# Gate scratch of a hybrid decoder step: from one block of memory per key group to one per pair of token blocks

## The reference

```python
s = einsum('thik,hink->thin', q, sub_keys)
s_top, i_top = top_k(s, 16)
cand = s_top[:, :, 0, :, None] + s_top[:, :, 1, None, :]
best_s, best_c = top_k(cand, 16)
eid = i1 * 128 + i2
g = softmax(best_s)
act = gelu(einsum('thkd,td->thk', u_tab[eid], tb))
out = einsum('thk,thkd->td', (g * act), v_tab[eid])
```

## Time and profile before

| | |
|---|---|
| Median of 3 runs | 2411.62 us (2409.38 to 2411.7) |
| The profiled execution's own time | 2407.87 us |
| Its span in the profile | 2406.0 us |
| PE busy | 2380.0 us (99%) |
| DVE, ACT, POOL busy | 1607.6, 837.2, 1432.2 us |
| Moved by DMA | 510.01 MB, mean 212 GB/s |
| `gate_scratch`: stores, loads | 56 of 512 KB; 30 of 896 KB and 2 of 832 KB |

### The profile page before, as it was taken

How to read it: one execution, slowest core, us unless ns; L and a number is a source line. 1 busy time by engine, 2 the same in 40 slices (tenths; PEclk the granted TensorE clock), 3 DMA queues, 4 the chain that set the end, 5 groups by cost and what they waited for, 6 DMA issues and landing times.

```text
span 2406.0 us, 38105 instructions
## 1 busy us (share of the span) xinstructions
PE 2380.0 (99%) x14550; PEld 2214.3 (92%) x14550; DVE 1607.6 (67%) x2611; ACT 837.2 (35%) x1279; POOL 1432.2 (60%) x787
## 2 busy tenths in 40 slices
PE   9999999999999999999999999999999999999998
PEld 8999999987899999999999999999989999999997
DVE  7865444455874353279897688888576766666664
ACT  4433223332231011233343355655433333333332
POOL 5554434332444555457676667777667777777762
PEclk9999999999999999999999999999999999999999
DMA  5224222237742233247776769999988888888872
GB/s 212 82 76 137 97 97 97 96 120 239 263 152 90 80 123 95 93 152 273 243 248 235 255 194 314 300 302 304 333 315 315 311 314 326 313 311 322 318 258 75
DMA packets 207742, 510.01 MB, mean 212 GB/s; under 512 B 15856, under 2 KB 104304, under 8 KB 205168
## 3 DMA queue, kind: packets, MB, share of 16 engines
q1 hardware_dynamic: 115552, 236.75, 30.9%
q10 hardware_dynamic: 55184, 137.07, 15.3%
q0 software_dynamic: 36864, 134.23, 15.0%
HBM read 424.55 MB, written 83.44 MB: 211 GB/s over the span
## 4 chain that ended last, share of the span: by engine, by line
PE 91%; DVE 5%; DMA 2%; ACT 1%; issue 1%; DVEq 0%; SPq 0%; ACTq 0%
PE ps L886 52%; PE ps L633 29%; PE ps L934 4%; DMA cxb<-parked_tiles 1%; DVE prev L1687 1%; PE ps L899 1%; PE ps L805 1%; PE ps L792 1%; PE ps L800 1%; PE ps L809 1%; PE ps L825 1%; PE ps L658 0%; DMA gbuf<-gate_scratch 0%; PE ps L778 0%; DVE hu_lo L1516 0%
## 5 line engine op out<-in xcount | busy, mean ns | idle before, releaser
L582 POOL TENSOR_SCALAR w_hi<-raw 128x1024 fp32r<-128x1024 f32 x129 | 138.9, 1076 | 520.8 <-issue 390.2
L609 POOL TENSOR_TENSOR w_lo<-raw,w_hi 128x1024 fp32r<-128x1024 f32 x128 | 324.3, 2534 | 188.3 <-PE ps L886 187.5
L609 POOL TENSOR_TENSOR w_lo<-raw,e_hi 128x1024 fp32r<-128x1024 f32 x128 | 324.5, 2535 | 177.8 <-PE ps L886 170.2
L886 PE MATMUL ps<-p_hi,w_lo 128*128 128x448 f32 x1024 | 376.2, 367 | 0.0
L886 PE MATMUL ps<-g_hi,w_lo 128*128 128x448 f32 x1024 | 375.6, 367 | 0.0
L584 POOL TENSOR_TENSOR w_lo<-raw,w_hi 128x1024 fp32r<-128x1024 f32 x129 | 318.5, 2469 | 10.8
L633 PE MATMUL ps<-h_hi,w_hi 128*128 128x296 f32 (+1 forms) x1216 | 274.3, 307 | 1.6 <-ACT ma L1201 1.6
L633 PE MATMUL ps<-h_lo,w_hi 128*128 128x296 f32 (+1 forms) x1216 | 262.5, 297 | 0.0
L633 PE MATMUL ps<-h_hi,w_lo 128*128 128x296 f32 (+1 forms) x1216 | 262.1, 297 | 0.0
L1295 ACT ACTIVATE e_hi<-raw 128x1024 fp32r<-128x1024 f32 x128 | 135.9, 1061 | 261.5 <-DMA raw<-units 120.4
L633 PEld LDWEIGHTS ps<-h_hi,w_hi 128*128 128x128 f32 x1216 | 196.1, 188 | 26.5 <-issue 23.8
(11 more groups left out here) (332 smaller groups left out, 5430.8 us busy)
## 6 DMA issues: line engine op xcount, KB each, us to landing
raw<-units SPq DMA_DIRECT2D x385, 512.0 KB
gate_scratch<-gt SPq DMA_DIRECT2D x56, 512.0 KB
activation_scratch<-ge ACTq DMA_DIRECT2D x120, 224.0 KB
abuf<-activation_scratch ACTq DMA_DIRECT2D x30, 896.0 KB, 5.8
gbuf<-gate_scratch ACTq DMA_DIRECT2D x30, 896.0 KB
prev<-ssm_in ACTq DMA_DIRECT2D x8, 1024.0 KB, 6.7
ssm_s<-prev ACTq DMA_DIRECT2D x8, 1024.0 KB, 4.5
parked_tiles<-stage ACTq DMA_DIRECT2D x24, 296.0 KB, 2.1
```

The lines of the kernel that those rows point to most:

```text
L582: pool.tensor_scalar(w_hi[:, s, :], raw[:, r, :], 1.0, 1.0, ALU.mult, ALU.mult).then_inc(s_whi, 1)
L609: pool.tensor_tensor(w_lo[:, n % 2, :], raw[:, n % RAW, :], e_hi[m % HS_].bitcast(F32), ALU.subtract)\
L886: last = mm(accp[par], w[:, k * P:(k + 1) * P], x_[:, k, t0:t0 + ND], start=k == 0 and i == 0, stop=k == KT - 1 and i == 2)
```

## The change

The DRAM tensor `gate_scratch` gets another order of dimensions: pair of token blocks, partition, key group, where it was key group, partition, pair of token blocks. The bytes, the tiles on the chip and the order and number of all instructions stay. A store now writes 8 key groups that lie behind one another: one run of 4096 bytes per partition, where it was 8 runs of 512 bytes. A load now reads one run of 512 bytes per partition and pair of blocks: 14 (13 for group 0) per partition, 2 MB apart, where it was one run of 7168 bytes (6656 for group 0).

```diff
-    gate_dram = nc.dram_tensor("gate_scratch", [2 * NG, P, NB // 2, GI // 2 * SB], F32).ap()
+    gate_dram = nc.dram_tensor("gate_scratch", [NB // 2, P, 2 * NG, GI // 2 * SB], F32).ap()
...
-                sp_.dma_start(gate_dram[gs, :, B].rearrange("g p a -> p g a"),
+                sp_.dma_start(gate_dram[B, :, gs],
                               gt[:, B % 2].rearrange("p (g i) t -> p g (i t)", g=2 * NG)[:, gs]).then_inc(s_gs[B % 2], 16)
...
                 act.dma_start(gbuf[:, hb, 0:blocks].rearrange("p b i t -> p b (i t)"),
-                              gate_dram[bass.ds(g * 2 + hb, 1), :, 0:blocks].rearrange("a p b i -> (a p) b i"))\
+                              gate_dram[0:blocks, :, bass.ds(g * 2 + hb, 1)].rearrange("b p a i -> p b (a i)"))\
                     .then_inc(s_gl[hb], 16)
```

## The result

| | before | changed |
|---|---|---|
| Median of 6 runs each | 2411.66 us | 2429.24 us |
| Lowest and highest | 2405.44 to 2416.41 | 2422.1 to 2433.66 |
| The profiled execution's own time, span | 2407.87, 2406.0 | 2433.66, 2431.6 |

The ratio is 1.0070, with a 95% interval from 1.0052 to 1.0087: slower by some 17 us, where 6.5 us were forecast. In a later measurement, of 6 more runs, the changed kernel had 2426.02 us, 1.0067 [1.0043, 1.0092]. Its profiled execution there took 2417.59 us with a span of 2415.7. That is 16 us from the one shown here, and the reason is part of what follows.

What follows compares the result with a forecast made beforehand. PE was taken to bound the kernel, busy for 2380.0 of 2406.0 us. Terms 0 + 5 + 1.5 + 0 = 6.5 us gave 2414.4 for the profiled execution and 2418 us against the median; range 2410.5 to 2440.

Steps and rivals of the forecast that it cites:

- rival 2: Gate loads, mainly second half: scattered runs 2 MB apart read slowly, much slower, 2475 us at 60 ns per packet; chance 0.20.
- The price of a packet: DMA queues: 27 ns per 512-byte packet, taken from the stores and assumed for the cut loads too.
- part 1: First-half stores: 1.27 us per store and engine in place of 1.73, DMA share about 0.86, worth 0 to PE.
- part 2: SP between the halves: holds at the last four stores vanish, weights issue sooner, putting three loads before the gate load.
- part 5: ACT's queue: even if half loads hold ACT 2.6 us, 30 times, slack of DVE and PE covers it: 0.
- Turn-taking packet by packet: DMA engines take queues in turn, one packet each, so the gate load, now with the smallest packets, is overtaken.
- Rival 1: Between the halves: small packets served in runs of some ten, load not starved, -2.5 to +2, 2411 us; chance 0.26.
- Part 3: First gate load between the halves: lands later behind other queues, 5 us of PE idle time, ends -2.5 and +7.
- Part 4: 28 half loads in the second half: some first halves land late, second halves cost nothing; 1.5 us, ends 0 and 8.

Runs made afterwards that it cites:

- near512: The kernel before with each 512-byte run padded by 64 unused bytes, so loads are cut in 512-byte runs lying side by side: 2419.41 us, 1.0051.
- odd_pitch: The changed kernel with 33 key groups in place of 32 in the tensor, so no power-of-two pitch: 2422.20 us, 1.0046.
- first_cut: The kernel before with only the two gate loads between the halves cut in 13 runs of 512 bytes: 2420.41 us, 1.0050, 4 runs.
- first_whole: The changed kernel with group 0's gates also stored and read back in the old order, so the two first loads are whole: 2418.84 us, 1.0028.
- after_early: The changed kernel with both gate loads between the halves issued earlier in ACT's program: 2419.77 us, 1.0040.
- after_filled: The changed kernel with 40 extra matmuls, results unread, on PE in front of the unit that waits: 2431.38 us, 1.0075.
- before_two_two: The kernel before with its last four stores issued in two pairs, a load of weights between: 2411.71 us, 0.9999.
- after_again: The changed kernel, unaltered, measured once more for comparison: 2426.02 us, 1.0067.
- before_early: The kernel before with both gate loads between the halves issued earlier in ACT's program: 2416.97 us, 1.0022.

## Why the prediction was partly right

**Where it was right.** The sign and the place were those forecast, and 2429.24 lies in the range. The latter is in part luck: the forecast's own terms with their upper ends, 2411.62 + 7 + 8, reach 2426.6, and what lies above was put in for rival 2, which fell. The change was forecast as 6.5 us and measured as 14 to 17.6. The price of a packet, 27 ns, was measured as 27 at the turn, and over the second half as (2488 - 1158) us over 46096 packets = 29 ns (2488 is 29.9% of 8320; 1158 is q10's part before without the gate loads). The stores were worth nothing (part 1), SP took 3.02 us for its four stores where some 2 were forecast and 7.18 were before (part 2), the DMA share was 0.87 and 0.90 where 0.86 and 0.91 were forecast, and ACT's issues of gate loads stayed at 0.4 to 0.6 us (part 5). Turn-taking packet by packet, the heart of the forecast, stands in the counts of 159, 154 and 157 and in the order of the packets on each engine.

**Rival 1 fell** with the same rows: were small packets served in runs, q10 would have several times as many as the others, and were every queue served in runs, the chains would show them. The rule of the Trainium skill that goes with it, "DMA: Bandwidth & Descriptors", section "Queues, rings and completion order", does not hold for the units that the profile counts as packets. **Rival 2 fell** too: at 27 to 30 ns there is no slow read, q10's share in the second half is 29.9% and not over 35, and `near512` and `odd_pitch` lose the same at the turn.

**Part 3 was too small.** It said that the wait "ends at 1733.2, that is 5.5 us later", and took 5 us. Measured, the load became 7.0 us longer (6.5 in the later profile). The wait ended 23.05 us behind the first of the four stores, where the sum has 21.5. Three terms of the sum make up most of these 1.5 us. First, 0.9 us were taken off because the rows were read as showing stores until about 1728.5. But the earlier trace rows end at 1729, and in the next us of the kernel before SP's queue is still full (440 of these packets are the stores' runs of 512 bytes):

```profile
q1 hardware_dynamic: 498, 0.40, 116.9%
```

The last store's packet starts at 1729.8, so the count for before, to 1729.4, was 0.4 too low, and nothing was to be taken off. Second, the packets that the engines moved from 1719.8 to the end of the load, counted in the trace of the changed kernel, take 20.4 us per engine and not 18.7: 94 packets of an earlier load of weights were not in the sum, those of 4096 bytes on q1 took 166 ns and not 159, those of 512 bytes 30. Third, in the other direction, the wait ended 0.5 us after the load's last packet started, at 1740.5, and not 1.9 after; the 1.9 came of reading the first load before as through at 1725.9, where its last packet starts at 1726.9. The sum also held nothing for the clock. With 1.37 us of idle time before, no row of before had shown it fall; with 8.39 us it fell to 0.50, which cost about 2.5 us (1.9 us of busy time at half speed and 5 at 0.68). In place of 5 us the turn costs 8.3 from the first of the four stores on (7.0 + 2.5, less the 1.2 that before lost behind the load), and 7.4 in the later profile (6.5 to PE's first matmul behind the load and 0.9 to the end).

**Part 4 was wrong in kind.** It took 1.5 us of a range from 0 to 8, and said that the second halves "have a further unit of 4.9 us in hand" and cost nothing. The load that starts the stall at 1973 is one of those: the load issued at 1931.18 is for the fifth unit of its group (the fourth product after the one that waits for it, at 1971.63, is the first of the next group). On DVE there is no further unit in hand: in the kernel before, the product falls due 16.1 us after the issue for second halves as for first ones. PE has the hand, and it is used up by DVE: a product that slips behind POOL's start takes 2.4 us, DVE has no idle time left, and the whole delay stands when the group ends. Nor was a delay of 1 or 2 us the right unit; what comes is 3.85 us of PE and 1.7 of clock, or nothing. Over the seven profiles with all thirty loads cut in 512 bytes, two of them the changed kernel's own, the second half is 6.0 us over 561.5 on average, and four of them are at 567 to 575. The six with whole loads there (before, `first_cut` and four more) average 0.5 over it, with one above 565. So some 8 at the turn and 6 behind are 14 of the 14 to 17.6 us measured; the prediction had 5 and 1.5.

Not all of the 6 can be put down to late gates. The seven profiles have seven stalls of 3.7 to 3.9 us, each costing some 5.5 with its clock. Four start with a late load of gates: the one at 1973, and one in `first_whole`, `after_early` and `after_filled`, where the first load of group 1 holds DVE for 4.7 to 5.0 us. Three start with late weights. With whole loads late gates start none in six profiles, and late weights start two (`first_cut`, `before_two_two`). That late weights come more often with cut loads is not shown by 3 in 7 against 2 in 6. What is common to the five by weights is the slip: `p_lo` waited 2.3 to 2.7 us for `p_hi`, took 2.3 to 2.6 us itself, and PE stood at the end of the group. Outside the stalls `p_lo` takes 0.62 to 0.63 us in the second half, even where it waited up to 2.0 us, and no stall follows. Nor is a late load of gates enough by itself: in `after_again`, `near512` and `odd_pitch` DVE waits 3.1 to 3.4 us for the one at 1786 to 1788, its product takes 0.62 us, and PE does not stand at all there.

**What stays open.** Why some executions of the same program have these late loads, of gates or of weights, and others none. Why a part before the first store, in which no gate is stored, differs by up to 9 us between profiles. And why `after_filled`, whose turn is shorter, is not faster; its profile has both of these, 6.5 us before the first store and two stalls. That the stalls which begin with a slip need POOL's subtraction at just that place was read from the rows and not tested by moving it.

## What to carry to other kernels

When queues take turns packet by packet, the length of one contiguous run is the priority of a transfer: cutting a load from 6656 to 512 bytes left its bytes alone, raised its engine time from 2.0 to 3.1 us, and made it 7 us later, and a transfer with large packets starves the small ones beside it, as `before_early` shows. So before cutting or joining runs, ask who waits for this transfer, what runs beside it, and how many packets each has; give the long runs to the side that someone waits for, here the load, even if the stores have slack and look expensive. And price a late wait by the engine's whole loop behind it: if a slip brings it into another engine's time, the slack can be gone for the rest of the group. When such a stall shows in one profile, look at what began it, and whether profiles without the change have it too, before putting it down to the change.

## What the runs showed of the hardware that was not expected

- After 8.39 us of idle PE the granted clock was 0.50 for the first matmuls and 0.68 in the 5 us behind; after 3.85 us it was 0.66 over 5 us. With dummy matmuls in the gap it stayed at 1.00.
- DVE's product of two SBUF tiles took 0.63 us alone. It took 0.97 us when it started 1.9 us after POOL's subtraction, and 2.42 when it started 0.46 us after it.

The first of these is read in rows shown above. For the second, the product at the turn, where POOL was not at work, is this row of the changed kernel; the 28 us before it, in which DVE has nothing else to do, hold the whole first load and the time ahead of its issue:

```profile
1741.28 0.63 DVE L2002 TENSOR_TENSOR abuf<-abuf,gbuf 128x448 f32<-128x448 f32 x1 [28.01 <-DMA gbuf<-gate_scratch]
```

- An issuing engine is held when much is outstanding in its queue: SP for 16.66 us on four stores of 512-byte runs while large packets ran beside them, but ACT for at most 0.6 us on its gate loads in the changed kernel's profile (0.7 in the later one), with 112 packets per engine in one load.
